# K pages turned in 32x32 blocks on VectorE and cached logits on 32x32 TensorE tiles

## What is computed

```python
z = h @ w_in                              # 2048 -> 4096: q, k, v, u
q, k, v, u = jnp.split(z, [ATTN_WIDTH, 2 * ATTN_WIDTH, 3 * ATTN_WIDTH], axis=-1)
k_mean = jnp.mean(kb, axis=2)             # blocks of 256 keys (two pages)
idx, valid = moba_select(q, q_pos, k_mean)  # per query and head the 3 best past blocks
s_sel = einsum(q, k_sel) * scale - slopes * dist   # cached logits
p = softmax(concat[s_sel, s_own]); o = p @ v_sel + p_own @ v_own
x = x + concat(o, pool_mixer(u)) @ w_out
x = x + (silu(h2 @ w_gate) * (h2 @ w_up)) @ w_down
```

## Time and profile before

| | |
|---|---|
| median of 3 runs | 1664.31 us (1663.76 to 1667.62) |
| span of the profiled execution | 1664.7 us |
| TensorE busy | 1571.4 us, 94% |
| VectorE / ScalarE busy | 766.7 us / 598.3 us |
| DMA, mean | 201 GB/s; 333.79 MB in all |
| matmuls of the weight tiles (L1170 to L1172), share of the chain that ended last | 79% |
| logits L1280 / values L1252, share of that chain | 6% / 4% |
| K turns L1176, busy | 162.8 us |
| ScalarE's copies of the turned K (L477), busy | 149.4 us |

### The profile page before, as it was taken

How to read it: one execution, slowest core, us unless ns; L and a number is a source line. 1 busy time by engine, 2 the same in 40 slices (tenths; PEclk the granted TensorE clock), 3 DMA queues, 4 the chain that set the end, 5 groups by cost and what they waited for, 6 DMA issues and landing times.

```text
span 1664.7 us, 33739 instructions
## 1 busy us (share of the span) xinstructions
PE 1571.4 (94%) x12884; PEld 1403.4 (84%) x12884; DVE 766.7 (46%) x1234; ACT 598.3 (36%) x874; POOL 104.6 (6%) x184
## 2 busy tenths in 40 slices
PE   5899999999999978898999999999999999999987
PEld 4776666666666656798999999999999999999986
DVE  3633233232332333555745555554545455465545
ACT  2423333332332343333543433333333334343333
POOL 1102161000000010000200000000000000000003
PEclk9998999999999998999999999999999999999998
DMA  5367889889889754655455555555555555555531
GB/s 178 111 230 243 308 314 333 296 297 339 315 296 339 279 177 148 200 179 152 139 166 164 164 164 164 157 172 164 164 165 164 165 164 162 169 165 156 176 128 57
DMA packets 154367, 333.79 MB, mean 201 GB/s; under 512 B 10463, under 2 KB 44312, under 8 KB 153727
## 3 DMA queue, kind: packets, MB, share of 16 engines
q1 hardware_dynamic: 154311, 333.05, 61.4%
HBM read 328.10 MB, written 5.27 MB: 200 GB/s over the span
## 4 chain that ended last, share of the span: by engine, by line
PE 91%; DVE 4%; ACT 2%; issue 2%; DMA 1%; POOL 0%; SPq 0%; DVEq 0%; POOLq 0%; ACTq 0%
PE bank L1170 24%; PE bank L1172 23%; PE bank L1171 23%; PE bank L1176 9%; PE bank L1280 6%; PE bank L1252 4%; DVE w_lo L685 1%; PE bank L1313 1%; ACT kT L477 1%; DMA vec<-in_pool_scale 1%; ACT w_hi L477 0%; PE bank L1346 0%; DVE nrm L701 0%; DVE d L773 0%; PE bank L1419 0%
## 5 line engine op out<-in xcount | busy, mean ns | idle before, releaser
L1170 PE MATMUL bank<-hh,w_hi 128*128 128x288 f32 x2176 | 658.6, 303 | 29.3 <-DVE w_lo L685 15.8
L1171 PE MATMUL bank<-hl,w_hi 128*128 128x288 f32 x2176 | 647.4, 298 | 0.0
L1172 PE MATMUL bank<-hh,w_lo 128*128 128x288 f32 x2176 | 645.2, 297 | 0.0
L685 DVE TENSOR_TENSOR w_lo<-w_raw,w_hi 128x1024 fp32r<-128x1024 f32 (+1 forms) x376 | 441.7, 1180 | 413.6 <-ACT w_hi L477 410.5
L477 ACT ACTIVATE w_hi<-w_raw 128x1024 fp32r<-128x1024 f32 x312 | 327.9, 1058 | 510.6 <-PE bank L1172 506.9
L1170 PEld LDWEIGHTS bank<-hh,w_hi 128*128 128x128 f32 x2176 | 413.2, 190 | 45.9 <-issue 34.9
L1172 PEld LDWEIGHTS bank<-hh,w_lo 128*128 128x128 f32 x2176 | 414.7, 191 | 0.0
L1171 PEld LDWEIGHTS bank<-hl,w_hi 128*128 128x128 f32 x2176 | 414.1, 190 | 0.1
L477 ACT ACTIVATE kT<-bank 128x512 f32<-128x512 f32 x256 | 149.4, 597 | 276.6 <-PE bank L1176 276.1
L1170 PE MATMUL bank<-ah,w_hi 128*128 128x288 f32 x704 | 210.4, 299 | 9.5 <-DVE af L1026 5.4
L1172 PE MATMUL bank<-ah,w_lo 128*128 128x288 f32 x704 | 210.4, 299 | 0.0
(11 more groups left out here) (177 smaller groups left out, 747.1 us busy)
## 6 DMA issues: line engine op xcount, KB each, us to landing
kpage<-in_cache_k SPq DMA_DIRECT2D x128, 512.0 KB, 5.7
vpage<-in_cache_v SPq DMA_DIRECT2D x128, 512.0 KB, 4.9
w_raw<-in_w_gate SPq DMA_DIRECT2D x88, 512.0 KB, 3.6
w_raw<-in_w_up SPq DMA_DIRECT2D x88, 512.0 KB, 3.6
w_raw<-in_w_down SPq DMA_DIRECT2D x88, 512.0 KB, 3.6
w_raw<-in_w_in SPq DMA_DIRECT2D x64, 384.0 KB, 6.6
w_raw<-in_w_out SPq DMA_DIRECT2D x32, 512.0 KB, 4.8
w_raw<-in_w_in SPq DMA_DIRECT2D x16, 512.0 KB, 4.4
```

The costliest lines, as they stand in the source:

```text
L685: V.tensor_tensor(w_lo[:, s, 0:width], w_raw[:, s, 0:width], w_hi[:, s, 0:width].bitcast(F32), ALU.subtract).then_inc(lo_ready, 1)
L1170: PE.matmul(o, wh, xh[:, c, :], start=start and i == 0, stop=False)
L1171: PE.matmul(o, wh, xl[:, c, :], start=False, stop=False)
L1172: last = PE.matmul(o, wl, xh[:, c, :], start=False, stop=stop and i == len(chunks) - 1)
```

## The change

K pages are no longer turned on TensorE. VectorE transposes each page in place, in 32x32 blocks (`turn_k`, four instructions of 128x1024 fp32 a quad, on four semaphores, one for each page). After that a partition holds, within a group of 32 tokens, one of 32 numbers of a head. The logits of a quad become 128 matmuls (`logits`): contraction over 32 partitions, 32 output rows, 128 columns (32 tokens of each of four pages), over the 16 tiles of a 4x4 grid of TensorE; the row group a of tokens goes to PSUM bank 2 + a. The four quads of a sequence are told apart by the offset into a zero-padded strip of queries, `qr`. For this the queries have to stand in all four groups of 32 partitions: a product with a repeated identity (`replicate_q`) and two copies do it once; `pad_q` places four columns for each sequence. The tables, `scaled_logits`, `select_blocks` and the running maxima follow the new layout; the maxima and sums are brought to 32 rows by one product at the end (`ml_in`).

The rest of the input projection has 256-column tiles of 1024 numbers a partition (512 rows of `w_in` by 256), 48 of them in the first six steps; steps 6 and 7 have none. ScalarE makes all high parts. The low part is written over the raw tile: `w_raw` and `w_lo` are the same memory, six slots, and `w_hi` has four. A load now waits for `w_used` of the tile six before, no longer for `lo_ready` of the tile four before. `kpage` no longer lies over `xs`; the first two quads of K are issued right after the q tiles. K is loaded two quads ahead, after `qk_done` of the quad in the same buffer; V keeps its single buffer. All loops of the cache stage and of the output projection are written out.

The core of the diff:

```diff
-T_OP = T_KVU + 8 * NB
+T_OP = T_KVU + 48
...
-CW = 384
-SLOTS = 4
+CW = 256
+RAW = 6
+HI = 4
...
-DVE_STEPS = 15
+KVU_STEPS = 6
+STRIP = 32
+PAD = 19
...
-        w_raw = sb("w_raw", [P, SLOTS, TE])
-        w_hi = sb("w_hi", [P, SLOTS, TE], F32R)
-        w_lo = sb("w_lo", [P, SLOTS, TE], F32R)
+        w_hi = sb("w_hi", [P, HI, TE], F32R)
+        raw = ExitStack()
+        w_raw = sb("w_raw", [P, RAW, TE], stack=raw)
+        raw.close()
+        w_lo = sb("w_lo", [P, RAW, TE], F32R)
...
-        WB = bank[0:3]
-        KTP = bank[3:5]
-        S = bank[5]
+        banks = ctx.enter_context(nc.psum_tensor("banks", [P, 8, 512], F32))
+        bank = [banks[:, n, :] for n in range(8)]
+        WB = bank[0:2]
+        S = banks[:, 2:6, 0:P]
...
-                    sp.wait_ge(lo_ready, n - 3)
+                    sp.wait_ge(w_used, n - RAW + 1)
...
-            def load_k(i, j, free=True):
-                if free:
-                    sp.wait_ge(kt_in, 32 * i + 8 * j - 8)
+            def load_k(i, j):
+                n = NQUADS * i + j
+                if n >= 2:
+                    sp.wait_ge(qk_done, n - 1)
                 for g in range(4):
-                    sp.dma_start(kpage[:, j % 2, g, :], page(ck, i, 4 * j + g)).then_inc(k_in[j % 2], 16)
-            def load_v(i, j, free=True):
-                if free:
-                    sp.wait_ge(v_done, 4 * i + j - 4)
+                    sp.dma_start(kpage[:, n % 2, g, :], page(ck, i, 4 * j + g)).then_inc(k_in[n % 2][g], 16)
+            def load_v(i, j):
+                n = NQUADS * i + j
+                if n:
+                    sp.wait_ge(v_done, n)
+                else:
+                    sp.wait_ge(xT_in, KC)
+                    sp.wait_ge(hist_T, 2)
                 for g in range(4):
-                    sp.dma_start(vpage[:, g, :], page(cv, i - 1, 4 * j + g)).then_inc(v_in, 16)
...
+            def load_kvu(n):
+                m, r = n // 4, n % 4
+                c0 = 4 * AW - CW * (m + 1)
+                load(tile_at(T_KVU + n), w_in_d[512 * r:512 * r + 512, c0:c0 + CW])
+            load_k(0, 0)
+            load_k(0, 1)
+            for i in range(NB):
                 for j in range(NQUADS):
-                    for k in (2 * j, 2 * j + 1):
-                        load(tile_at(T_KVU + k, i, 8), w_in_d[256 * k:256 * k + 256, bass.ds(i * (-CW) + (4 * AW - CW), CW)])
-                    if j < NQUADS - 1:
-                        load_k(i, j + 1, not (j == 0 and not has_v))
-                    elif next_k:
-                        load_k(i + 1, 0)
-                    if has_v:
-                        load_v(i, j, not (first_v and j == 0))
...
+                    if i < KVU_STEPS:
+                        load_kvu(8 * i + 2 * j)
+                        load_kvu(8 * i + 2 * j + 1)
+                    ahead = NQUADS * i + j + 2
+                    if ahead < NQUADS * NB:
+                        load_k(ahead // NQUADS, ahead % NQUADS)
+                    if i:
+                        load_v(i - 1, j)
...
+            def hi_kvu(i, j):
+                if i < KVU_STEPS:
+                    for k in (2 * j, 2 * j + 1):
+                        hi(tile_at(T_KVU + 8 * i + k))
...
+                    act.wait_ge(comb_done, b)
+                copy(osb[:, 0:512], OB[0][:, :]).then_inc(o6_taken, 1)
+            for i in range(NB):
+                hi_kvu(i, 0)
+                if i >= 2:
+                    save_comb(i - 2)
+                if i >= 1:
+                    softmax_late(i - 1)
+                for j in range(1, NQUADS):
+                    hi_kvu(i, j)
+                if i >= 1:
+                    osb_low(i - 1)
...
-            def lo(t, width=TE):
-                n, _, s = t
+            def lo(t):
+                n, _, s, u = t
                 dve.wait_ge(hi_ready, n + 1)
-                V.tensor_tensor(w_lo[:, s, 0:width], w_raw[:, s, 0:width], w_hi[:, s, 0:width].bitcast(F32),
+                V.tensor_tensor(w_lo[:, s, :], w_raw[:, s, :], w_hi[:, u, :].bitcast(F32),
                                 ALU.subtract).then_inc(lo_ready, 1)
-            def hi_lo(t):
-                n, turn, s = t
-                dve.wait_ge(w_in_s[s], 16 * turn + 16)
-                dve.wait_ge(w_used, n - 3)
-                V.tensor_copy(w_hi[:, s, 0:2 * CW], w_raw[:, s, 0:2 * CW]).then_inc(hi_ready, 1)
-                lo(t, 2 * CW)
...
+            own.link(V.memset(qr[:, :], 0.0))
+            dve.wait_ge(sq_added, KC)
+            V.tensor_copy(rep_w, ident.rearrange("p (c i) -> p c i", c=4).unsqueeze(2).to_broadcast([P, 4, 4, 32])
+                          ).then_inc(rep_table, 1)
+            dve.wait_ge(rep_in, 1)
+            for x in range(2):
+                V.tensor_copy(qrep[:, 16 * x:16 * x + 16, :],
+                              OB[x].rearrange("p (s t) -> p s t", t=TS)).then_inc(rep_taken, 1)
+            dve.wait_ge(rep_taken, 2)
             def pad_q(b):
-                cols = bass.ds(TP + NQ * b, NQ)
-                return V.tensor_copy(qz[:, :].rearrange("p (h s) -> p h s", s=36)[:, :, 0:NQ], z[:, ZQ:ZQ + H, cols])
-            def scaled_logits(i, has_comb):
-                if has_comb:
-                    dve.wait_ge(pt_in, i - 1)
-                own.did(V.scalar_tensor_tensor(ss[:, :, :].rearrange("p j k -> p (j k)"), S[:, :], SCALE, past_bias,
-                                               ALU.mult, ALU.add))
-                own.did(V.tensor_reduce(d4[:, :], S[:, :].rearrange("p (j k) -> p j k", j=4), AX.X, ALU.add))
+                V.tensor_copy(qr[:, PAD:PAD + 32 * STRIP].rearrange("p (s q w) -> p s q w", s=32, q=8)[:, :, 0:NQ, 0],
+                              qrep[:, :, NQ * b:NQ * b + NQ]).then_inc(qr_ready, 1)
+            def turn_k(i, j):
+                n = NQUADS * i + j
+                for g in range(4):
+                    dve.wait_ge(k_in[n % 2][g], 16 * (n // 2) + 16)
+                    V.transpose(kpage[:, n % 2, g, :], kpage[:, n % 2, g, :]).then_inc(k_turned, 1)
...
+            def take_block(m):
+                dve.wait_ge(w_used, T_KVU + 4 * m + 4)
+                for e in range(2):
+                    V.tensor_tensor(z[:, ZU + 6 - 2 * m + e, :], WB[e][:, 0:T], rstd[:, :],
+                                    ALU.mult).then_inc(z_ready, 1)
...
+                V.tensor_copy(osb[:, 512:1024], OB[1][:, :]).then_inc(o7_taken, 1)
+            pad_q(0)
+            turn_k(0, 0)
+            for i in range(NB):
+                lo_kvu(i, 0)
+                if i:
+                    select_blocks(i - 1)
+                    joint_max(i - 1)
+                turn_k(i, 1)
+                if i:
+                    joint_sum(i - 1)
+                lo_kvu(i, 1)
+                turn_k(i, 2)
+                if i < KVU_STEPS:
+                    take_block(2 * i)
+                lo_kvu(i, 2)
+                turn_k(i, 3)
+                lo_kvu(i, 3)
+                if i < NB - 1:
+                    scaled_logits(i)
+                    pad_q(i + 1)
+                    turn_k(i + 1, 0)
+                if i < KVU_STEPS:
+                    take_block(2 * i + 1)
+                if i:
+                    osb_high(i - 1)
...
+            def replicate_q():
+                pe.wait_ge(rep_table, 1)
+                for c in range(2):
+                    pe.wait_ge(quad_taken[c], QT0)
+                for c in range(4):
+                    last = PE.matmul(OB[c // 2][:, 256 * (c % 2):256 * (c % 2) + 256],
+                                     rep_w[:, c, :, :].rearrange("p a i -> p (a i)"), z[:, ZQ:ZQ + H, TP:T],
+                                     start=True, stop=True)
+                last.then_inc(rep_in, 1)
...
+                    for n in range(4):
+                        last = PE.matmul(OB[x][32 * n:32 * n + 32, :], pT[:, n, bass.ds(j, 32, 4)],
+                                         vpage[:, n, 512 * x:512 * x + 512], start=j == 0, stop=j == NQUADS - 1)
...
+            def logits(b, j):
+                n = NQUADS * b + j
+                pe.wait_ge(k_turned, 4 * n + 4)
+                if j == 0:
+                    pe.wait_ge(qr_ready, b + 1)
+                    if b:
+                        pe.wait_ge(dn_ready, b)
+                for hh_ in range(2):
+                    for c in range(4):
+                        for a in range(4):
+                            for x in range(4):
+                                h = 4 * hh_ + x
+                                at_ = STRIP * (8 * c + h) + PAD - j - 16 * hh_
+                                k = DH * h + 32 * c
+                                last = PE.matmul(S[32 * x:32 * x + 32, a, :], qr[32 * a:32 * a + 32, at_:at_ + 32],
+                                                 kpage[32 * a:32 * a + 32, n % 2, :, k:k + 32],
+                                                 start=j == 0 and hh_ == 0 and c == 0,
+                                                 stop=j == NQUADS - 1 and hh_ == 1 and c == 3)
```

(61 more changed lines are left out.)

381 lines of the change are left out of this document (142 added, 239 removed).

## The result

The changed kernel takes 1784.65 us (1783.51 to 1788.64, 4 runs) against 1665.96 us for the kernel before: ratio 1.0701, 95% interval 1.0676 to 1.0725. The profiled execution has a span of 1781.9 us.

A forecast was written before the change was run, and what follows sets the result against it. TensorE sets the cache stage's pace, DMA a second floor right under it; after the change 113.6 + 420 + 17 + 6.4 + 3.4 = 560.4 against 597.6, 37 us less: 1627 us, range 1590 to 1690.

The forecast's parts named there:

- The transposes: VectorE, cache stage: each 128x1024 transpose of a K page takes 1.23 us, 4.9 us a quad.
- Sixteen tiles at once: TensorE, a quad's logits: sixteen 32x32 tiles run side by side, 2.2 us a quad, taken as 3.0.
- The column-groups rival: Logits on TensorE: only column groups run side by side, 64 rounds, 7.4 us a quad; chance 13%.
- Fetching the logits' instructions: TensorE, cache stage: fetching 32 KB of instructions a quad is covered by the margin within the 3.0 us for logits.
- the four-wide rival: Cache stage: only column groups run side by side, TensorE sets the pace, stage ends at 617, 1684 us; chance 13%.
- A full queue at 347 GB/s: DMA, cache stage: 145.7 MB left after the first logits move at 347 GB/s, 420 us, plus holes at step ends.
- Start: Cache stage from 100.8: clearing, replicating queries, copies, padding, four transposes and first logits, done at 113.6.
- tail: After the cache stage: loads waiting for use, six slots deep, cost nothing, 3 us either way.
- What would show it: Signs: logits 2.2 to 3.7 us a quad, TensorE idle before values, DMA share above 0.92, last values near 560.

The follow-up runs named there:

- `e_burst_loop`: Changed kernel, four raw slots, seven of eight logits product groups in each step's second quad, one in others, TensorE's steps 2 to 5 as a loop; 1730.67 us.
- `e_loop`: Changed kernel with TensorE's steps 2 to 5 as a loop, four raw slots instead of six and a product with zeros ahead of the logits; 1855.97 us.
- `e_b_unroll`: Kernel before the change with TensorE's loop over steps 2 to 7 written out, nothing else; 1669.65 us, ratio 1.0005.
- `e_half`: Changed kernel with only half of the logits' products (heads 0 to 3), 256 instructions a quad; 1675.0 us.
- `e_burst`: Changed kernel, written out, four raw slots, seven of eight logits product groups in each step's second quad and one in the others; 1749.41 us.
- the best repaired version: Changed kernel with logits in halves, weight tiles a quad earlier, V before K, last values, turned probabilities and VectorE's turning of quad 1 moved; 1707.73 us.

## Why the prediction was wrong, point by point

Forecast were 1627 us, in a range of 1590 to 1690, and so a gain of 37 us in the cache stage; measured are 1784.65 and a loss of 112 us there.

- **The transposes**: right, 1.23 us taken, 1.213 measured, the pace of the subtraction over the same width (1.226). The trace sides with one element per cycle and lane in the Trainium skill (Vector Engine (DVE) Microarchitecture Reference, section 3.8), and not with the 2.5 us estimated from the Trainium skill (VectorE: DVE Perf Modes, The three transpose paths).
- **Sixteen tiles at once**: right. The changed kernel's one quad without a gap takes 3.73 us, and at the 12.9 ns a matmul of `e_burst_loop` (224 in 2.89 us) a quad would take 3.3: near the 3.0 taken. It is also near the 2.7 estimated from the Trainium skill (TensorE: Matmul & The Clock Gate, Part 3). The column-groups rival is out as a mechanism: that a quad came out near its 7.4 us is chance.
- **Fetching the logits' instructions: the step that failed.** I wrote down the 32 KB a quad and covered them with a margin of 0.8 us, by the volume of all packets. Volume was the wrong view; the rate against the burst decides. The term measured (139.1 + 90.1)/32 = 7.2 us a quad instead of 3.0, with 2.8 us of it in holes. Writing out the loops, which I had costed at nothing, made no difference by itself: a step of 164 KB is fetched again in a loop too (`e_loop`). The Trainium skill (Runtime: NRT & Kernel Launch, Instruction fetch mechanics) says that TensorE's instructions come in 16 KiB blocks of 256, that a new block is mostly hidden because dispatch is slower than filling, and that full unrolling is preferred where possible. The block agrees (packets of 16384 bytes). The hiding holds in `e_b_unroll`, where 256 instructions take 13 us, and not here, where `e_half` starts 256 of them in 1.6 us and a block takes about 3.5. Nor did writing out pay for the 79 KB step: `e_burst` is 19 us slower than `e_burst_loop`.
- **What it set off.** With such a quad I had the four-wide rival at 1684 and a step at 67.6 us, and the kernel is 100 us slower than that. The steps from 251.6 and 331.3 us take 79.7 and 78.0, of which TensorE's busy time and its holes are 74 and 73. Values took 3.4 us a quad (107.7/32) instead of 1.9, with a granted clock of 0.83 from 100 to 600 us. The clock by itself is not the cause: `e_half` is granted 0.83 there as well. The transfers slow down with TensorE, because K is issued after the logits before it and V after the values before it: 247 GB/s from 100 to 600 us, against 295 in `e_half`. The 63 us of waits for V are not a second loss. `e_half`, without any hole, waits longer for V, because there the transfers set the pace, as forecast:

```profile
L1276 PE MATMUL banks<-vpage,pT 128*32 128x512 f32 x512 | 90.8, 844 | 99.3 <-DMA vpage<-in_cache_v 99.3
```
- **A full queue at 347 GB/s**: right where TensorE kept up, and only in steps 1 to 5. In `e_half` these five last 316.7 us at 330 GB/s, against 319 by my sum (5 x (40 x 1.51 + 3.4)). From the end of the first logits the first step took 48 instead of 33 (22 x 1.51), the last two 122.0 instead of 94. There V's single buffer has a period of its own, which I had put at 12.1 (the transfers alone). Its values stand 13.3 and 13.6 us apart, with a wait for V before each, in `e_half`:

```profile
558.02 3.65 PE L1276 MATMUL banks<-vpage,pT 128*32 128x512 f32 x16 [2.33 <-DMA vpage<-in_cache_v]
...
571.35 3.65 PE L1276 MATMUL banks<-vpage,pT 128*32 128x512 f32 x16 [7.61 <-DMA vpage<-in_cache_v]
...
584.91 3.65 PE L1276 MATMUL banks<-vpage,pT 128*32 128x512 f32 x16 [7.73 <-DMA vpage<-in_cache_v]
```
  So even without the stalls the sum had 40 us too little: `e_half` ends its last values at 601.8, not at 560.4, and 1675 us would have been no gain.
- **Start** (first logits done at 113.6 forecast; they begin at 109.9 and end at 116.5) and **tail** (3 us either way; 5.3 more): nearly right. The tail needs the six slots; four cost 55 to 61 us in five kernels.
- **What would show it**: the signs worked. A quad's logits were to take 2.2 to 3.7 us; 31 of 32 took 5.1 to 9.1. The DMA share was to be above 0.92; it was 0.74 from 120 to 540 us. And GB/s stayed under 305 (259 there) though TensorE and DMA both had time to spare. Idle time before the values was there, so that sign alone would have passed the forecast; holes inside the logits I had not named.

Open: the best repaired version stays at 1707.73 us, 2.3% above the kernel before (1.0205 to 1.0259). Its waits are spread over V (40.9 us), the turned K (43.2) and issue (19.5); no run parts these. Whether a second V buffer would bring it under the kernel before wasn't tried.

## What to carry to other kernels

Before replacing few large matmuls by many small ones, count instructions in a burst and set 14 ns each against the time that they run: up to 256 in a row were free here, 512 cost 2.8 us on average and at most 4.6. Put slow instructions (large matmuls) between the pieces, and look at what the loads behind them wait for before moving anything. A loop helps such bursts where its body is kept (79 KB was, 120 KB was not); without bursts it gained nothing (`e_b_unroll`).

## What the runs showed of the hardware beyond expectation

- Gaps by length of burst, written out: 256 instructions 0 of 32 quads, 320 in 7 of 32, 448 in 6 of 8, 512 in 31 of 32. That fits between one and two packets being there when a burst begins; it is an inference from these counts.
- Instruction packets keep a distance: the closest two start 3.4 us apart in the changed kernel's cache stage and 3.2 in that of `e_loop`, though each moves for about 1 us only. That they are fetched one at a time is an inference.
- A loop of 120 KB is slower than the same written out (1780.12 against 1760.22 us, 2 runs each).
